# Two layers of attention: difference and band heads among the last input tiles, latent heads among half tiles of the output projection

## The chip, the cores and the metric

The kernel runs on one core of one Trainium2 chip. The metric is the device time of one execution in microseconds (us), as the median of several runs. Its engines are called by their names in the profile: PE is TensorE (PEld its weight loads), DVE VectorE, ACT ScalarE, POOL GpSimd, SP the engine that issues most of the loads. Each has its own queue of instructions, worked off in order.

## The reference

A network of two parts on 256 tokens of width 2048, in float32. The first part has two layers. Of each layer (`first_block`):

```
h = rms_norm(x); proj = h @ w_in              # 30 column tiles of 128: c_q (3), c_kv, k_rope, then q, k, v of B and of C
out_a = mla_mixer(...)                        # 8 latent heads; q and k, v come from c_q @ w_uq and c_kv @ w_ukv
out_b = diff_mixer(...)                       # 4 difference heads, two score maps each, a norm behind them
out_c = chunk_band_mixer(...)                 # 4 band heads with a learned bias
x = x + concat(out_a, out_b, out_c) @ w_o     # output projection, 2048 x 2048
h = rms_norm(x)
x = x + square(relu(h @ w_up)) @ w_down       # 2048 -> 8192 -> 2048
```

The second part (`second_block`) is one layer with a sliding window, a diagonal state space (SSM) and an MLP of the same size. The change doesn't touch its work. The tables of its state space are computed by POOL and ACT beside the two layers of the first part.

## The kernel before

Weights come as chunks of 2 MB (`raw[0]`, `raw[1]`, loaded by SP in turns). A chunk is two tiles. For float32 accuracy every tile is split: ACT copies it into a rounded high part (`w_hi`, two halves of 1024 columns), DVE subtracts to get the low part (`w_lo`), and PE multiplies high by high, high by low and low by high. There are two buffers of high and low parts. So the split of tile T+2 waits on ACT until PE has ended tile T (`tile_done`), and the load of a chunk waits until the chunk before it in its buffer is split.

Of a layer l, in PE's order:

- 30 input tiles (`tile`), whose results DVE folds and scales into `proj` (`project`).
- The "fills": 14 groups of float32 matmuls for w_uq and w_ukv (`uq_done`), read out by ACT (`uq_out`, L1251). Groups 0 to 5 are the long ones. The chunks that follow in the weight buffers wait for them: SP loads chunk 18 (the first of w_o) behind fill 5, chunk 19 behind fill 13.
- 16 transposes of the values of B and C (L810).
- 20 score units in a software pipeline of steps s: units 0 to 7 of the difference heads, 8 to 11 of the band heads, 12 to 19 of the latent heads. PE does `scores(s)`, the transposes of unit s-2 (`turn`), and the product with the values of unit s-3 (`values`). DVE does bias and maxima (`biased`), sums and scaling one step later (`normed`), and the low part of the output five steps later (`act_lo`, L1747). ACT does the exponentials (`exps`, L1264), `weights_out` and the high part of the output (L1280). `values` of a latent head waits for the low part of the output of two heads before (`olo_ready`), since both use one bank of PSUM.
- 16 tiles of the output projection (`wide`), four for each 512 columns, each over a quarter of the rows of w_o. DVE adds each 512 columns to x (`added`, L1577), and PE turns them (`turn_x`, L690) for the next norm.
- The MLP: 16 up tiles and 16 wide down tiles, four times.

Beside this runs the preparation of the SSM. POOL begins `ssm_powers` when all heads of the layer are out (L2056 at its start), and waits in its middle for a sine and cosine that ACT computes in `before_mlp(1)` (L1303 to L1310). `before_mlp(c)` stands in ACT's queue behind the first split that follows the first tile of 512 columns c+1. Behind `ssm_powers` POOL builds the phases (L2172 is the signal that they are ready), then the matrices. Only then does it come to `hidden` (L2207), the low parts of the MLP's hidden tiles. ACT's queue holds this for the MLP:

```
def ffn(T0, c2, H0, each=None, i0=None):
    with act.Fori(0, FCH - 1) as f:
        if i0 is not None:
            ssm_trig_table(i0 + f)            # waits for POOL's phases
        ups(T0, c2, f, H0)
...
def up(T0, c2, f, q, t, H0, to_wide=False):
    T = T0 + 2 * T_UP * f + 4 * q + t
    act.wait_ge(hlo_ready, H0 + T_UP * f + 4 * q + t + 1)   # up tile 2 needs POOL's first hidden tile
    low_to(T, t, hid[t][:])                                 # L1125
...
        split(T + 2, c2 + C_UP * f + q + (t // 2 + 1) // 2, (1 + t // 2) % 2, t % 2)
```

Of the kernel before, what the change touches and what calls it, by code (L numbers as in the profile page):

```python
# [16 lines left out]
F32 = mybir.dt.float32  # L17
# [110 lines left out]
def build(nc, stream, params, tables, tables2, cbias, xrow, gfin, metaT, smat, out, stabs, urow, yrow):  # L128
# [102 lines left out]
    assert side_end <= region[0] - 4 * HC * 384  # L231
# [6 lines left out]
    vb = place("vb", [P, 2, HB * P], where=region)  # L238
    vc = place("vc", [P, 2, HC * P], where=region)
    sb0 = place("sb0", [P, 384], where=region)  # L240
    nmax = [place(f"nmax{i}", [P, 2], where=region) for i in range(2)]
    psums = [place(f"psums{i}", [P, 2], where=region) for i in range(2)]
    rsums = [place(f"rsums{i}", [P, 2], where=region) for i in range(2)]
    nlr = place("nlr", [P, 2], where=region)
    sb = [sb0, sb1]
# [5 lines left out]
    rt = place("rt", [P, 4, 2, S], where=region)  # L251

# [8 lines left out]
    ob, osq, ostd, orstd = proj[:, VB:VB + 4, :], proj[:, VC:VC + 4, :], proj[:, 0:4, :], proj[:, KC:KC + 4, :]  # L261
# [50 lines left out]
    with ExitStack() as ctx:  # L312
# [184 lines left out]

        def gated_tiles(t):

            return [4 * (t // 2) + 2 * e + t % 2 for e in range(2)]  # L500
# [24 lines left out]
        def _(sp):  # L525
# [11 lines left out]
            with sp.Fori(0, DEPTH) as l:  # L537
# [96 lines left out]
        def _(pe):  # L634
# [48 lines left out]

            def turn_x(n, c):
# [83 lines left out]
            with pe.Fori(0, DEPTH) as l:  # L768
# [11 lines left out]
                pe.wait_ge(const_ready, 1)  # L780
                pe.wait_ge(tab_landed, 16)

                pe.wait_ge(cn_ready, l + 1)
# [6 lines left out]
                for n, (c, ws, j0) in enumerate(tiles):  # L790
                    if n in (0, 6, 12):
                        pe.wait_ge(landed[c % 2], chunk_landed(l * C2_LAYER + c // 2))
                    if n % 2 == 0 and n >= 8:
                        pe.wait_ge(uq_out, 14 * l + n // 2 - 3)
                    for k, w in enumerate(ws):
                        last = mm(bank[4 + n // 2 % 4][:, 256 * (n % 2):256 * (n % 2) + 256], w, proj[:, j0 + k, :],
                                  k == 0, k == len(ws) - 1)
                    if n % 2 == 1:
                        last.then_inc(uq_done, 1)
                for g in range(4):  # L800
                    pe.wait_ge(uq_out, 14 * l + 10 + g - 3)
                    c0 = 1024 + 512 * (g % 2)
                    mm(bank[4 + (10 + g) % 4][:], proj[:, QT, 128 * (g // 2):128 * (g // 2) + 128], flat[1][:, c0:c0 + 512], True, True)\
                        .then_inc(uq_done, 1)

                pe.wait_ge(evac_done, evacuated(T0 + T_O - 1))
                pe.wait_ge(uq_out, 14 * l + 14)
                for g, v0 in enumerate((VB, VB, VC, VC)):
                    for h in range(4):
                        last = pe.transpose(bank[4 + g][:, 128 * h:128 * h + 128],  # L810
                                            proj[:, v0 + h, 128 * (g % 2):128 * (g % 2) + 128], ident)
                    last.then_inc(vt_done, 1)

                def scores(u):
# [3 lines left out]
                    else:  # L819
                        pe.wait_ge(vt_out, 4 * l + 4)  # L820
# [19 lines left out]
                def turn(g, u):  # L840
                    pe.wait_ge(pn_ready, GROUPS * l + g + 1)
                    if g >= 2:
                        pe.wait_ge(pt_ready, GROUPS * l + g - 1)
                    for i in range(3):
# [3 lines left out]
                def values(g):  # L848
                    pe.wait_ge(pt_ready, GROUPS * l + g + 1)
                    if 2 <= g < 2 + HB:  # L850
                        pe.wait_ge(osq_ready, HB * l + g - 1)
# [3 lines left out]
                    o = bank[g % 2]  # L855
# [3 lines left out]
                for s in range(UNITS + 3):  # L859
# [1609 lines left out]
```

## Time and profile before

| | |
|---|---|
| median of 3 runs | 3306.08 us (3301.94 to 3314.55) |
| the profiled execution | 3318.74 us |
| its span, first to last instruction | 3316.9 us |
| mean granted clock of PE | 0.973 |
| busy share of the span | PE 98%, DVE 56%, ACT 45%, POOL 19% |
| the chain that ended last | PE 92%, ACT 2%, issue 2%, DVE 2%, DMA 1% |
| head stage of layer 0, last input tile to output projection | 197.25 to 307.07 us |

### The profile page before, as it was taken

Reading aid. Unit: us, or ns where it says so; the run is one execution under the profiler, and the core shown is the slowest. Engines: PE = TensorE matmul, PEld = TensorE weight load, DVE = VectorE, ACT = ScalarE, POOL = GpSimd, SP = SyncE. Lnnn points to the kernel's source line nnn. Section 1 sums busy time; section 2 is a strip of 40 time slices with the busy share of each in tenths; the row PEclk is TensorE's granted clock in tenths of the full one; section 3 lists DMA queues with packets and bytes.
Section 4 is the critical chain, followed back from the end, with each engine's and each line's share of the span. In section 5 each row is a group of like instructions: output and inputs, shape, how many; then the busy total and the mean of one; then the engine's idle time right before and its main releaser. Section 6 shows DMA issues by size and latency. Waiting matters only on the chain.

```text
span 3316.9 us, 46606 instructions
## 1 busy us (share of the span) xinstructions
PE 3235.5 (98%) x16696; PEld 2735.7 (82%) x16696; DVE 1840.9 (56%) x2381; ACT 1493.9 (45%) x2319; POOL 640.7 (19%) x701
## 2 busy tenths in 40 slices
PE   8989999999999999899999999999899999999999
PEld 6877888888888888688888888889866888888887
DVE  5645655565555563656655555557555655555554
ACT  4344553545444443445444444452454544434343
POOL 1011513141411111044414031114110010101010
PEclk9987999999999999699999999999989999999999
DMA  6440456564555545145645555567422455555554
GB/s 227 177 177 34 178 187 223 180 224 182 215 194 211 186 179 190 39 160 181 225 181 210 199 206 203 211 221 261 149 77 102 178 192 189 192 188 195 185 193 162
DMA packets 66281, 602.11 MB, mean 182 GB/s; under 512 B 13968, under 2 KB 24464, under 8 KB 31072
## 3 DMA queue, kind: packets, MB, share of 16 engines
q1 hardware_dynamic: 54560, 592.33, 48.9%
q10 hardware_dynamic: 11184, 5.49, 0.6%
q0 software_dynamic: 400, 2.44, 0.2%
q8 instruction: 87, 1.43, 0.2%
q14 instruction: 50, 0.41, 0.0%
HBM read 582.09 MB, written 18.15 MB: 181 GB/s over the span
## 4 chain that ended last, share of the span: by engine, by line
PE 92%; ACT 2%; issue 2%; DVE 2%; DMA 1%; POOL 0%; SPq 0%; ACTq 0%; DVEq 0%; POOLq 0%
PE bank L638 90%; DMA raw<-stream 1%; PE bank L690 1%; ACT w_hi L1085 0%; DVE w_lo L1534 0%; PE bank L845 0%; DVE w_lo L1528 0%; DMA urow<-us 0%; POOL cssb L2218 0%; DMA u<-urow 0%; PE bank L735 0%; ACT prob L1264 0%; PE bank L970 0%; DVE sb L1714 0%; DVE nmax L1724 0%
## 5 line engine op out<-in xcount | busy, mean ns | idle before, releaser
L638 PE MATMUL bank<-xg,w_hi 128*128 128x512 f32 (+1 forms) x4544 | 1544.7, 387 | 13.8 <-DVE w_lo L1534 10.1
L638 PE MATMUL bank<-xg,w_lo 128*128 128x256 f32 (+1 forms) x4352 | 1228.5, 282 | 0.0
L638 PEld LDWEIGHTS bank<-xg,w_hi 128*128 128x128 f32 x4544 | 849.6, 190 | 195.8 <-DVE w_lo L1534 8.2
L1528 DVE TENSOR_TENSOR w_lo<-raw,w_hi 128x1024 fp32r<-128x1024 f32 x480 | 625.7, 1341 | 520.3 <-ACT w_hi L1096 520.3
L638 PEld LDWEIGHTS bank<-xg,w_lo 128*128 128x128 f32 x4352 | 825.1, 190 | 0.7
L1096 ACT ACTIVATE w_hi<-raw 128x1024 fp32r<-128x1024 f32 x480 | 482.3, 1054 | 660.4 <-PE bank L638 660.4
L1534 DVE TENSOR_TENSOR w_lo<-raw,w_hi 128x1024 fp32r<-128x1024 f32 x548 | 680.2, 1247 | 160.1 <-ACT w_hi L1085 159.7
L638 PE MATMUL bank<-w_hi,act_hi 128*128 128x512 f32 x1920 | 753.5, 392 | 1.9 <-DVE act_lo L1747 1.9
L638 PE MATMUL bank<-w_hi,act_lo 128*128 128x512 f32 x1920 | 749.5, 390 | 0.0
L638 PE MATMUL bank<-w_lo,act_hi 128*128 128x512 f32 x1920 | 749.2, 390 | 0.0
L1085 ACT ACTIVATE w_hi<-raw 128x1024 fp32r<-128x1024 f32 x552 | 552.5, 1052 | 167.5 <-PE bank L638 164.5
L2207 POOL TENSOR_TENSOR act_lo<-hid,act_hi 128x256 f32 x192 | 193.4, 1007 | 1467.8 <-ACT act_hi L1136 1467.8
L638 PEld LDWEIGHTS bank<-w_hi,act_hi 128*128 128x128 f32 x1920 | 361.7, 188 | 82.7 <-issue 6.1
L638 PEld LDWEIGHTS bank<-w_hi,act_lo 128*128 128x128 f32 x1920 | 361.6, 188 | 75.8
L638 PEld LDWEIGHTS bank<-w_lo,act_hi 128*128 128x128 f32 x1920 | 362.0, 189 | 74.0
L1603 DVE TENSOR_TENSOR hid<-bank,hid 128x256 f32<-128x256 f32 x192 | 81.6, 425 | 372.0 <-ACT hid L1125 372.0
L1125 ACT ACTIVATE hid<-bank 128x256 f32<-128x256 f32 x192 | 73.8, 385 | 390.8 <-PE bank L638 390.7
L1136 ACT ACTIVATE act_hi<-hid 128x256 f32 (+1 forms) x192 | 80.6, 420 | 147.8 <-DVE hid L1613 147.8
L1579 DVE SCALAR_TENSOR_TENSOR x<-bank,stats,x 128x512 f32<-128x512 f32 x96 | 67.7, 747 | 90.5 <-issue 77.5
L1125 ACT ACTIVATE proj<-bank 128x256 f32 (+1 forms) x60 | 23.1, 384 | 193.8 <-PE bank L638 193.8
L1603 DVE TENSOR_TENSOR proj<-bank,proj 128x256 f32 (+1 forms) x60 | 25.3, 422 | 111.1 <-ACT proj L1125 110.6
L1613 DVE SCALAR_TENSOR_TENSOR hid<-hid 128x256 f32<-128x256 f32 x192 | 82.9, 432 | 0.0
(311 smaller groups left out, 1934.6 us busy)
## 6 DMA issues: line engine op xcount, KB each, us to landing
raw<-stream SPq DMA_DIRECT2D x264, 2048.0 KB, 7.7
stabs<-ssm_tabs SPq DMA_DIRECT2D x8, 1176.0 KB, 9.8
rdo<-stabs SPq DMA_DIRECT2D x8, 768.0 KB, 8.7
ssm_bc<-smat SPq DMA_DIRECT2D x8, 640.0 KB, 11.9
stabs<-ssm_f SPq DMA_DIRECT2D x8, 512.0 KB, 11.0
drv<-stabs SPq DMA_DIRECT2D x8, 512.0 KB, 5.5
trig<-stabs SPq DMA_DIRECT2D x8, 408.0 KB, 9.7
x<-xrow SPq DMA_DIRECT2D x4, 512.0 KB, 7.2
```

The costliest lines, as they stand in the source:

```text
L638: return pe.matmul(o, a, b, start=start, stop=stop, skip_group_check=True)
L690: last = pe.transpose(bank[4 + k % 4][:, P * m:P * m + P], x[:, m, P * k:P * k + P], ident)
L1085: act.activation(hi[j][:, 8 * h:8 * h + 8, :], raw[r][:, 8 * h:8 * h + 8, P * j:P * j + P], ACT.Copy)\
L1096: act.activation(flat_hi[j][:, 1024 * h:1024 * h + 1024], flat_raw[r][:, 2048 * j + 1024 * h:2048 * j + 1024 * h + 1024], ACT.Copy).then_i ...
L1125: act.activation(dst, bank[b][:, S:2 * S], ACT.Copy).then_inc(low_out, 1)
L1136: act.activation(act_hi[:, bass.ds(4 * q + t, 1), :], hid[t][:].rearrange("p (a n) -> p a n", a=1), ACT.Copy)\
L1528: dve.tensor_tensor(flat_lo[j][:, 1024 * h:1024 * h + 1024], flat_raw[r][:, 2048 * j + 1024 * h:2048 * j + 1024 * h + 1024], flat_hi[j][:, ...
L1534: dve.tensor_tensor(lo[j][:, 8 * h:8 * h + 8, :], raw[r][:, 8 * h:8 * h + 8, P * j:P * j + P], hi[j][:, 8 * h:8 * h + 8, :].bitcast(F32), ...
L1579: dve.scalar_tensor_tensor(out=one, in0=bank[2 * (c % 2) + m][:], scalar=rs2[:, m:m + 1], in1=one, op0=ALU.mult, op1=ALU.add).then_inc(eva ...
L1603: return dve.tensor_tensor(dst, bank[b][:, 0:S], dst, ALU.add).then_inc(folded, 1)
L1613: dve.scalar_tensor_tensor(out=one, in0=one, scalar=0.0, in1=one, op0=ALU.max, op1=ALU.mult).then_inc(evac_done, 1)
L2207: pool.tensor_tensor(act_lo[:, bass.ds(4 * q + t, 1), :], hid[t][:].rearrange("p (a n) -> p a n", a=1), act_hi[:, bass.ds(4 * q + t, 1), : ...
```

## The change

In both layers of the first part the order of the work is written anew. The difference and band units go one by one behind the input tiles 18 to 28, their last steps among the fills. The latent units go among eight tiles of the output projection that need only the rows of the difference and band heads (rows 1024 on), in half tiles (`out_half`) on a list, m counting the latent steps. Eight more tiles for the rows of the latent heads follow, two for each 512 columns, so that each 512 columns are added to x twice. The chunks of w_o are laid out for it on the host. The tiles 18 to 29 and the fills use two banks of PSUM. SP's load of the SSM's matrices moves behind the seventh chunk of w_o. POOL's code is the same, and so are `before_mlp`, `ffn` and `up`.

```diff
+        FILLS = {11: (2,), 12: (3,), 13: (4,), 14: (5,), 15: (6, 7, 8, 9), 16: (10, 11, 12, 13)}
+        OUT_HALVES = {1: (0,), 2: (1,), 3: (2, 3), 4: (4, 5), 5: (6, 7), 6: (8, 9), 7: (10, 11), 8: (12, 13), 9: (14,), 10: (15,)}
+        OUT_SPLITS = {0: 0, 1: 1, 2: 2, 3: 3, 4: 4, 5: 5, 6: 6, 7: 7, 8: 8, 10: 9}
+        OUT_ADDED = {4: 0, 6: 1, 8: 2, 11: 3}
...
-                pair(0, first_matrices)
-                with sp.Fori(0, 7) as q:
-                    pair(2 + 2 * q)
+                pair(0)
+                pair(2)
+                pair(4, first_matrices)
+                with sp.Fori(0, 5) as q:
...
+            def out_half(T, t, h, b, k0):
+
+                pe.wait_ge(lo_ready, lo_count(T, h))
+                for i in (2 * h, 2 * h + 1):
+                    k = k0 + 4 * t + i
+                    for m in range(2):
+                        o = bank[b + m][:]
+                        a_hi, a_lo = (v[:, k, P * m:P * m + P] for v in (act_hi, act_lo))
+                        mm(o, a_hi, wide_hi[t][:, i, :], t == 0 and i == 0, False)
+                        mm(o, a_hi, wide_lo[t][:, i, :], False, False)
+                        last = mm(o, a_lo, wide_hi[t][:, i, :], False, t == 1 and i == 3)
+                if h == 1:
+                    last.then_inc(tile_done, 1)
+
...
-                with pe.Fori(0, 6) as q:
+                with pe.Fori(0, 3) as q:
...
+                def fill(i):
+
+                    if i < 2:
+                        pe.wait_ge(evac_done, evacuated(T0 + T_O - 2 + i))
+                    else:
+                        pe.wait_ge(uq_out, 14 * l + i - 1)
+                    if i == 0:
+                        pe.wait_ge(const_ready, 1)
+                        pe.wait_ge(tab_landed, 16)
+                        pe.wait_ge(cn_ready, l + 1)
+                    if i < 10:
+                        for n in (2 * i, 2 * i + 1):
+                            c, ws, j0 = tiles[n]
+                            if n in (0, 6, 12):
+                                pe.wait_ge(landed[c % 2], chunk_landed(l * C2_LAYER + c // 2))
+                            for k, w in enumerate(ws):
+                                last = mm(bank[i % 2][:, 256 * (n % 2):256 * (n % 2) + 256], w, proj[:, j0 + k, :],
+                                          k == 0, k == len(ws) - 1)
+                    else:
+                        c0 = 1024 + 512 * (i % 2)
+                        last = mm(bank[i % 2][:], proj[:, QT, 128 * ((i - 10) // 2):128 * ((i - 10) // 2) + 128], flat[1][:, c0:c0 + 512],
...
+                for j in range(12):
+                    T = T0 + 18 + j
+                    tile(T, j % 2, j % 2, None, evacuated(T - 2))
+                    if j == 0:
+                        pe.wait_ge(evac_done, evacuated(T0 + VB + 3))
+                        for g in range(2):
+                            turn_values(g)
+                    unit_step(j - 1, 0, MLA0)
+                    if j in (7, 9, 11):
+                        sums((j - 7) // 2)
+                for i in range(2):
+                    fill(i)
+                pe.wait_ge(evac_done, evacuated(T0 + T_O - 1))
+                pe.wait_ge(pt_ready, GROUPS * l + 5)
...
+                for s in range(11, 17):
+                    if s == 12:
+                        sums(3)
+                    unit_step(s, 0, MLA0)
+                    for i in FILLS[s]:
+                        fill(i)
...
+                for m in range(UNITS - MLA0 + 3):
+                    unit_step(MLA0 + m, MLA0, UNITS)
+                    for w in OUT_HALVES.get(m, ()):
+                        if w in (0, 1):
+                            pe.wait_ge(onlo_ready, HB * l + 2 * w + 2)
+                        if w == 0:
+                            pe.wait_ge(ostd_ready, 5 * l + HB)
+                            pe.wait_ge(olo_ready, OTHERS * l + HC)
+                        elif w % 4 == 0:
+                            pe.wait_ge(evac_done, evacuated(T0 + T_O + w // 2 - 1))
+                        out_half(T0 + T_O + w // 2, w // 2 % 2, w % 2, 2, 8)
+
+                pe.wait_ge(pt_ready, GROUPS * l + GROUPS)
+                for c in range(NC):
+                    if c % 2:
+                        pe.wait_ge(evac_done, evacuated(T0 + T_O + 8 + 2 * c - 3))
+                    for t in range(2):
+                        for h in range(2):
+                            if c == 0:
+                                pe.wait_ge(olo_ready, OTHERS * l + HC + 4 * t + 2 * h + 2)
+                            out_half(T0 + T_O + 8 + 2 * c + t, t, h, 2 * (c % 2) if c else 6, 0)
+                        if c and t == 0:
+                            pe.wait_ge(evac_done, evacuated(T0 + T_O + 8 + 2 * c - 1))
+                            turn_x(2 * l + 1, c - 1)
                 ffn(T0 + T_FFN, l * H_LAYER, 2 * l + 1, 2 * l + 2, FCH * l)
...
+                for m in range(UNITS - MLA0 + 4):
+                    unit_step(MLA0 + m, MLA0, UNITS)
+                    if m in OUT_SPLITS:
+                        out_split(OUT_SPLITS[m])
+                    if m == 0:
+                        for h in range(HB):
+                            act.wait_ge(on_ready, HB * l + h + 1)
+                            act.activation(act_hi[:, 8 + h, :], ob[:, h, :], ACT.Copy).then_inc(onhi_ready, 1)
...
-                widened(T0 + T_O, c0 + 9, before_mlp)
+                for c in range(NC):
+                    for t in range(2):
+                        i = 8 + 2 * c + t + 2
+                        (split_wide if i < 16 else split)(T0 + T_O + i, c0 + 9 + i // 4, i // 2 % 2, t)
+                        if c and t == 0:
+                            before_mlp(c - 1)
+                before_mlp(NC - 1)
...
+                def unit_step(s, a, b):
+
+                    if max(a, CB0) <= s - 5 < b:
+                        output_low(s - 5)
+                    if s - MLA0 in OUT_ADDED and a == MLA0:
+                        c = OUT_ADDED[s - MLA0]
+                        half_added(T0 + T_O + 2 * c + 1, c, 2)
+                    if a <= s < b:
+                        if s == CB0:
+                            dve.wait_ge(cb_landed, 16 * l + 16)
                         biased(s)
-                    if 1 <= s < UNITS + 1:
+                    if a <= s - 1 < b:
...
+                for m in range(UNITS - MLA0 + 5):
+                    unit_step(MLA0 + m, MLA0, UNITS)
+                    if m in OUT_SPLITS:
+                        out_split(OUT_SPLITS[m])
+                    if m == 0:
+                        for h in range(HB):
+                            normed_low(h)
...
-                widened(T0 + T_O, lambda c: gained(2 * l + 1, c, "mlp_g", l * KT))
+                for c in range(NC):
+                    for t in range(2):
+                        T = T0 + T_O + 8 + 2 * c + t
+                        i = 8 + 2 * c + t + 2
+                        if t == 1:
+                            half_added(T, c, 2 * (c % 2) if c else 6)
+                        for h in range(2):
+                            if i < 16:
+                                split_wide_half(T + 2, i // 2 % 2, t, h)
+                            else:
+                                split_half(T + 2, i // 2 % 2, t, h)
+                            if c == NC - 1 and t == 1 and h == 0:
+                                gained(2 * l + 1, NC - 1, "mlp_g", l * KT)
+                        if c and t == 0:
+                            gained(2 * l + 1, c - 1, "mlp_g", l * KT)
```

## Rows read from the trace of the kernel before

**Rows 1.** The page's second part, TensorE's clock in 40 slices, in tenths.

```profile
PEclk9987999999999999699999999999989999999999
```

**Rows 2.** The windows, 20 us, layer 0 (PE, PEld, DVE, ACT, POOL, clock, DMA, GB/s).

```profile
280.00:300.00 20.00, 20.00 (x58) 13.69 (x56) 13.56 (x30) 6.14 (x24) 0.00 (x0) 0.50 0.00 1
```

**Rows 3.** The timeline of PE, layer 0 (start, us, engine, line, operation).

```profile
220.87 1.97 PE L810 MATMUL bank<-tab,proj 128*128 128x128 f32 x16 [0.69 <-ACT va L1251]
...
238.61 1.65 PE L638 MATMUL bank<-proj 64*128 64x128 f32 x4
...
260.97 0.39 PE L638 MATMUL bank<-kn,qn 128*128 128x128 f32 x2
...
263.61 0.55 PE L845 MATMUL bank<-tab,prob 128*128 128x128 f32 x3
...
264.00 0.82 PE L638 MATMUL bank<-probT,vc 128*128 128x256 f32 x4
...
264.65 1.89 PE L638 MATMUL bank<-proj,ones 128*128 128x256 f32 x8
...
307.07 0.50 PE L638 MATMUL bank<-w_hi,act_hi 128*128 128x512 f32 x1 [0.93 <-DVE act_lo L1747]
```

**Rows 4.** The timeline of ACT, layer 0, input and head stages.

```profile
197.25 0.38 ACT L1125 ACTIVATE proj<-bank 128x256 f32<-128x256 f32 x1 [5.20 <-PE bank L638]
...
212.79 0.60 ACT L1251 ACTIVATE qn<-bank 128x512 f32<-128x512 f32 x1 [1.99 <-PE bank L638]
...
234.09 0.19 ACT L1264 ACTIVATION_READ_ACCUMULATOR prob<-sb,nmax 128x1 f32 x1
```

**Rows 5.** The timeline of DVE, same stretch.

```profile
232.06 0.55 DVE L1714 SCALAR_TENSOR_TENSOR sb<-tab,bank 128x384 f32<-128x384 f32 x1
```

**Rows 6.** The instructions of tile act_lo (ns minimum/median/maximum).

```profile
L1747 DVE TENSOR_TENSOR act_lo<-bank,act_hi x24: 417/424/426, 262.9 to 1408.7; 128x256 fp32r<-128x256 f32 x24
```

**Rows 7.** The page's sixth part: issues, KB, us to landing.

```profile
raw<-stream SPq DMA_DIRECT2D x264, 2048.0 KB, 7.7
```

**Rows 8.** The timeline of PE, second block, at a wait.

```profile
2456.91 0.90 PE L970 MATMUL bank<-tab,prob 128*128 128x128 f32 x3 [2.36 <-DVE prob L1971]
```

**Rows 9.** The windows, 2.5 us, behind that wait.

```profile
2457.50:2460.00 2.50, 2.50 (x11) 1.14 (x10) 2.12 (x8) 1.61 (x7) 0.84 (x3) 0.50 0.95 406
```

**Rows 10.** The timeline of ACT, layer 0, output projection and first up tiles.

```profile
357.29 2.01 ACT L1096 ACTIVATE w_hi<-raw 128x1024 fp32r<-128x1024 f32 x2 [3.43 <-PE bank L638]
...
379.94 2.01 ACT L1096 ACTIVATE w_hi<-raw 128x1024 fp32r<-128x1024 f32 x2 [3.44 <-PE bank L638]
...
386.30 2.01 ACT L1096 ACTIVATE w_hi<-raw 128x1024 fp32r<-128x1024 f32 x2 [1.68 <-PE bank L638]
...
404.75 1.28 ACT L1163 ACT_TABLE_LOAD   x1
...
417.06 0.39 ACT L1125 ACTIVATE hid<-bank 128x256 f32<-128x256 f32 x1 [0.47 <-PE bank L638]
```

**Rows 11.** The timeline of DVE, output projection.

```profile
358.38 2.36 DVE L1528 TENSOR_TENSOR w_lo<-raw,w_hi 128x1024 fp32r<-128x1024 f32 x2 [2.91 <-ACT w_hi L1096]
...
374.57 1.29 DVE L1577 TENSOR_TENSOR x<-bank,x 128x512 f32<-128x512 f32 x2 [1.91 <-PE bank L638]
```

**Rows 12.** The timeline of PE, third up tile.

```profile
411.16 0.50 PE L638 MATMUL bank<-xg,w_hi 128*128 128x512 f32 x1 [1.62 <-DVE w_lo L1534]
```

**Rows 13.** The timeline of POOL, output projection, up tiles, and one later build.

```profile
307.10 0.56 POOL L2056 TENSOR_TENSOR ssm_t<-par 128x32 f32<-128x32 f32 x2 [95.49 <-DVE act_lo L1747]
...
361.31 0.26 POOL L2056 TENSOR_TENSOR ssm_lpow<-ssm_mag,ssm_cs 128x32 f32<-128x32 f32 x1 [41.97 <-ACT ssm_cs L1310]
...
389.42 1.06 POOL L2172 COPY consts<-consts 128x1 f32<-128x1 f32 x1
...
413.87 0.74 POOL L2207 TENSOR_TENSOR act_lo<-hid,act_hi 128x256 f32 x1
...
515.11 0.19 POOL L2172 COPY consts<-consts 128x1 f32<-128x1 f32 x1
```

More of the change, by code:

```diff
@@ L789, in _ @@
                 tiles += [(17, [flat[1][:, 128 * t:128 * t + 128]], QT) for t in range(HA)]
[L790 to L808, printed above, removed]
+                def fill(i):
[18 more added lines that the diff above has]
+                        last = mm(bank[i % 2][:], proj[:, QT, 128 * ((i - 10) // 2):128 * ((i - 10) // 2) + 128], flat[1][:, c0:c0 + 512],
+                                  True, True)
+                    last.then_inc(uq_done, 1)
@@ new lines, in _ @@
+                for j in range(12):
+                    project(18 + j, j % 2)
+                    if j < 10:
+                        split(T0 + 20 + j, c0 + (20 + j) // 4, (20 + j) // 2 % 2, j % 2)
+                    if j == 0:
+                        for g in range(2):
+                            values_turned(g)
+                    unit_step(j - 1, 0, MLA0)
+                    if j in (8, 10):
+                        sums_out((j - 8) // 2)
+                for i in range(2):
+                    fill_out(i)
@@ new lines, in _ @@
+                for g in range(2, 4):
+                    values_turned(g)
+                sums_out(2)
+                for s in range(11, 17):
+                    if s == 12:
+                        sums_out(3)
+                    unit_step(s, 0, MLA0)
+                    if s == 13:
+                        act.wait_ge(ostd_ready, 5 * l + HB)
+                        act.activation(ostd, ostd, ACT.Sqrt, bias=eps, scale=1.0 / P).then_inc(ostd_ready, 1)
+                    for i in FILLS[s]:
+                        fill_out(i)
@@ new lines, in normed_low, with out_split, half_added @@
+                def normed_low(h):
+                    dve.wait_ge(onhi_ready, HB * l + h + 1)
+                    dve.tensor_tensor(act_lo[:, 8 + h, :], ob[:, h, :], act_hi[:, 8 + h, :].bitcast(F32), ALU.subtract)\
+                        .then_inc(onlo_ready, 1)
+                def out_split(i):
+                    for h in range(2):
+                        split_wide_half(T0 + T_O + i, i // 2 % 2, i % 2, h)
+                def half_added(T, c, b):
+                    dve.wait_ge(tile_done, multiplied(T))
+                    for m in range(2):
+                        one = x[:, m, W * c:W * c + W]
+                        dve.tensor_tensor(one, bank[b + m][:], one, ALU.add).then_inc(evac_done, 1)
```

209 lines of the change are left out of this document (94 added, 115 removed).

## The prediction

> **What bounds the kernel now.** I read the page's busy shares first, then TensorE's clock beside them, then the windows and timelines of the stages the diff touches. PE is the chain: outside two stretches it is dense and its clock is full. The clock in slices [rows 1] shows two dips, in the third and fourth slices and in the 17th, which are the head stages of the two layers. In the second half of the latent units PE is busy for all 20 us of a window and gets 0.50, the 1.2 GHz level [rows 2]. So the busy share hides the loss: work lies there that costs twice. The stage lasts from the last input tile (197.25 [rows 4]) to the first tile of the output projection (307.07 [rows 3]), 109.8 us. The projection behind it goes without a gap.
>
> **What the stage holds at full clock.** Fills: from 197.25 to 220.18, the end of ACT's last read-out in front of the transposes (220.87 less the idle 0.69 [rows 3]), 22.9. Transposes 2.0 [rows 3]. One latent step, scores 2.64 (260.97 to 263.61), transposes 0.39, values 0.65, is 3.68, eight of them 29.4 [rows 3]. A difference score took 1.65 at the lower level [rows 3], so 0.83; eight of these with four transposes and values make 11. Four band units, a score as dear, 7.4. The sums of the norm 1.9 [rows 3]. Sum 74.6. Hidden gaplessly between tiles that PE runs anyway, the change would take 109.8 - 74.6 = 35.2 us off each layer. I charge 2 for some 20 more switches between kinds of work at about 0.1.
>
> **Input stage.** Behind each of 11 tiles (5.58 apart: 5.20 idle and 0.38 on ACT [rows 4]) stands one unit, 1.2 to 1.9 on PE. A split holds ACT for 2.0 [rows 10] and DVE until 3.45 after a tile's end (358.38 + 2.36 - 357.29 [rows 10, 11]); with fold, scaling, bias, maxima and one unit's sums DVE is done some 6.4 after it, inside 7 to 7.5. The next split is ready a whole tile ahead. I expect no stall. Two banks in place of four hold too, since a tile's bank is free before its neighbour ends.
>
> **First half of the projection, step by step.** A tile is 5.43 and a turn of x 0.93: four tiles and one turn lie between 357.29 and 379.94, one of each between 379.94 and 386.30 [rows 10]. A half is 2.72. I count from the end of the last fill.
>
> Junction, m=0 and 1. PE does two scores, to 5.3. Its first half tile needs, in a row: scores 2.64; bias to exponentials 2.2 (232.06 to 234.28 [rows 4, 5]); then, because `out_split(0)` stands behind `exps(12)` in ACT's queue, the split, 3.45; then two low parts of difference heads behind it on DVE, 0.7. That is 9.0, so PE idles 3.7. Chunk 18 is no later: it is asked for behind fill 5, lands in 7.7 [rows 7], and the eight fills after take about 7.4 (212.79 to 220.18 [rows 4]). An idle of 2.36 in the second block [rows 8] was followed by a window at 0.50 [rows 9]; restarting I charge 2.5 here. Junction 6.2.
>
> Steps m=4 to 9. The split of tile w+2 waits for the end of tile w, and in DVE's queue it stands ahead of the next step's work. So after each step's last half tile DVE is free at 3.45, has the low part of a head at 3.87 (0.42 [rows 6]) and an addition to x at 5.16 (1.29 [rows 11]). PE wants the low part when scores and transposes are done, at 3.03, and the addition (before halves 4, 8, 12) after values.
> - m=4: addition at 4.74 against 3.68: 1.1.
> - m=5 and 7: 0.85 each.
> - m=6: 0.85, values to 4.52, addition 5.16: 1.5.
> - m=8: no scores are left, PE asks at 0.39: 3.5, values to 4.5, addition 5.16: 4.1.
> - m=9: 3.5, because `out_split(8)` has DVE again.
> Together 11.9, and 2 for the clock behind the two long gaps. Steps 10 and the latent half of the projection I cost at nothing: there splits (3.45) and additions (1.29) fit in a tile of 5.43. If DVE slipped there by more than 0.7, each slip would show on PE.
>
> The saving is 35.2 - 2 - 6.2 - 13.9 = 13.1 per layer. The eight additions more, 1.29 each, cost only what stands above.
>
> **What the diff doesn't touch but moves.** `before_mlp(1)` still stands behind the first tile of the third 512 columns. Before, seven tiles of the projection are left then; now the columns have two tiles, and three are left. Relative to the end of the projection, E (379.94 + 0.93 + 3 x 5.43 = 397.16 [rows 10]), sine and cosine come four tiles later, 21.7. What hangs on them:
> - POOL starts again at 361.31, 35.9 before E, signals the phases at 390.48 and is free for `hidden` at 413.87, 52.6 after its start [rows 13]. It will start 14.1 before E.
> - ACT wants the phases at 404.75, E+7.6 [rows 10]: the cover was 14.3. Moved unchanged they come at E+15.
> - Up tile 2 wants POOL's first hidden tile at 417.06 [rows 10]; it is there at 414.6, a cover of 2.4. Moved unchanged it is there at E+39.2.
> POOL needn't be so long: its signal took 1.06 in this stretch and 0.19 in another [rows 13], beside DVE's splits. Nine operations of such a length lie behind the phases' start, 0.87 apiece; DVE stands idle while PE waits, so I give back 5.5 and keep 0 and 8.1 as ends. Hidden tile 0 is then ready at E+33.7. Behind it: ACT 0.39, split half 1.05, DVE half 1.2, so up tile 4 starts at E+36.3. Before, tile 2 started at 411.16 [rows 12], E+14.0, and tile 4 two tiles of 5.6 later, E+25.2. The loss is 11.1, and 1.8 for a cold start: 12.9 per layer. On the way ACT's wait for the phases opens the gap in front of up tile 2 from 1.62 to about 7, inside the same sum. POOL's first part, 12.2 long (307.10 to 319.3, [rows 13]), still ends well ahead of the cosine.
>
> The Trainium skill says of POOL's slow operations (SBUF — State Buffer, "Who interferes with whom") that a DVE instruction with two SBUF inputs contends with a GpSimd instruction that reads SBUF, and that the one that comes second waits for the whole of the first. The signal's 1.06 against 0.19 agrees.
>
> **Sum.** 13.1 gained, 12.9 lost, twice: -0.4 us. The profiled execution would go from 3318.7 to 3318.3. It lies 12.7 above the median of the runs shown, by which the forecast is 3306.
>
> **Rivals.**
> - A, the preparation stays hidden. For it: POOL might be much faster beside an idle DVE. Against: 21.7 us against covers of 14.3 and 2.4. The loss of 12.9 falls away: 3306 - 26 = 3280.
> - B, the queues in steps 4 to 9 don't bite, since DVE or ACT run ahead of my order. For it: in the second block, head steps among half tiles leave PE few gaps. Against: the waits are in the order of the queues. 13.9 less: 3278.
> - C, the slower side: the clock. In the old stage the latent units never brought it back alone [rows 2]. If the idle at the junction puts PE to 1.2 GHz and m=1 to 3 all stay there, the half of m=1 costs 2.7 more, m=2 5.7 (scores, transposes, half), m=3 9.1: 17.5, where I charged 2.5. That is 15 per layer, 3336. It decides from 8.3 us per layer on, about two such steps. The Trainium skill (TensorE: Matmul & The Clock Gate, "HAM oscillation — how this bites in real kernels") tells of kernels whose bursts alternate with waits and start cold every time, which is this rival; the dip behind the wait in the second block agrees, and the full clock of the slices after it [rows 1] speaks against its lasting.
> - D, POOL isn't shortened: 5.5 more per layer, 3317, inside the middle.
> - E, both A and B and no junction, 66 off: 3240.
>
> **Numbers.** The forecast with D 0.45, A 0.13, B 0.13, E 0.04, C 0.16, and 0.09 for a lag in the input stage that no row shows. Its own range is 3294 to 3319: per layer POOL's ends give +5.5 and -2.6, the clock charges (2.5, 2 and 1.8, each between 0 and twice) up to 3 or so either way. With A and B on one side and C on the other, 3278 to 3336. A measurement of this kernel can tell about 0.5%, 16.5 us. Faster 0.30 (A, B, E), same 0.45, slower 0.25.
>
> **What would show it.** The head units among the input tiles without PE idle; the clock at 1.00 there. An idle of 3 to 4 in front of the first half tile of w_o. In steps 8 and 9 two gaps of 3 to 4 ended by `act_lo`. ACT waiting for POOL at the first table of the MLP, and up tile 4 starting 35 to 38 us after the end of the projection, in both layers. I am wrong if that time stays near 25, if the eight first tiles and units take far from 93 us (29.4 + 8 x 5.43 + 6.2 + 13.9) from the last fill, or if the clock is low through the latent steps.

## The result and the profile after

| | before | changed |
|---|---|---|
| median, 13 runs each, side by side | 3304.64 us (3292.72 to 3315.91) | 3320.98 us (3312.94 to 3324.87) |
| profiled execution | 3318.74 us | 3324.87 us |
| mean granted clock in it | 0.973 | 0.980 |

The ratio is 1.0041 [1.0027, 1.0055]: slower by 16 us, where I forecast no change. Forty-three more runs of the kernel before, beside the experiments, put its median over 56 runs at 3306.1 us. The profiled executions differ by 6.1 us only; the forecast was -0.4 for them. So there are two things to explain: 6.5 us in the sum for the profiled executions, and some 9 us more by which the medians lie apart (the changed kernel's median is 3.9 below its profiled execution, that of the kernel before 12.7).

PE's clock in 40 slices, the changed kernel. The dip to 6 of [rows 1] is gone:

```profile
PEclk9998999999999999999999999999989999999999
```

PE's timeline in layer 0, every wait from the first half tile of w_o to up tile 4 (the idle time in brackets):

```profile
251.34 0.79 PE L651 MATMUL bank<-w_hi,act_hi 128*128 128x512 f32 x1 [3.62 <-DVE act_lo L1865]
...
276.96 0.49 PE L651 MATMUL bank<-w_hi,act_hi 128*128 128x512 f32 x1 [1.14 <-DVE x L1878]
...
286.57 0.92 PE L651 MATMUL bank<-probT,va 128*128 128x256 f32 x4 [0.85 <-DVE act_lo L1836]
...
296.85 0.92 PE L651 MATMUL bank<-probT,va 128*128 128x256 f32 x4 [0.85 <-DVE act_lo L1836]
...
298.12 0.49 PE L651 MATMUL bank<-w_hi,act_hi 128*128 128x512 f32 x1 [0.35 <-DVE x L1878]
...
309.32 1.65 PE L651 MATMUL bank<-probT,va 128*128 128x256 f32 x4 [0.86 <-DVE act_lo L1836]
...
320.96 0.92 PE L651 MATMUL bank<-probT,va 128*128 128x256 f32 x4 [3.54 <-DVE act_lo L1836]
...
322.24 0.66 PE L651 MATMUL bank<-w_hi,act_hi 128*128 128x512 f32 x1 [0.37 <-DVE x L1878]
...
333.45 1.65 PE L651 MATMUL bank<-probT,va 128*128 128x256 f32 x4 [3.54 <-DVE act_lo L1836]
...
406.83 0.80 PE L651 MATMUL bank<-xg,w_hi 128*128 128x512 f32 x1 [4.92 <-DVE w_lo L1632]
...
426.88 0.80 PE L651 MATMUL bank<-xg,w_hi 128*128 128x512 f32 x1 [6.64 <-DVE w_lo L1632]
```

These rows answer to [rows 3] and [rows 12]. The reader is to see the junction (3.62; I had 3.7), the steps m=4 to 9 (1.14, 0.85, 0.85 and 0.35, 0.86, 3.54 and 0.37, 3.54, together 11.5; I had 11.9), and two waits at the MLP's start where [rows 12] has one of 1.62. The windows of the same phase (length, PE busy, clock, DMA share, GB/s) show what the idle sums don't:

```profile
242.00:252.00 10.00, 6.38 (x27) 0.77 0.57 210
252.00:262.00 10.00, 10.00 (x36) 0.72 0.37 123
...
282.00:292.00 10.00, 9.14 (x44) 1.00 0.06 23
292.00:302.00 10.00, 8.79 (x34) 0.83 0.44 152
302.00:312.00 10.00, 9.14 (x38) 0.84 0.13 57
...
322.00:332.00 10.00, 7.66 (x27) 0.83 0.47 190
332.00:342.00 10.00, 8.55 (x27) 0.66 0.01 2
342.00:352.00 10.00, 10.00 (x45) 1.00 0.40 132
```

ACT's timeline, layer 0: the last fill read out, the split behind the eighth tile, which ends the first half, the split at the projection's end E (in [rows 10] this is at 397.16 by the count, 7.5 later), and the wait for the phases:

```profile
242.34 0.60 ACT L1307 ACTIVATE va<-bank 128x512 f32<-128x512 f32 x1 [0.36 <-PE bank L651]
...
343.40 2.01 ACT L1155 ACTIVATE w_hi<-raw 128x1024 fp32r<-128x1024 f32 x2 [7.88 <-PE bank L651]
...
389.63 2.01 ACT L1144 ACTIVATE w_hi<-raw 128x1024 fp32r<-128x1024 f32 x2 [1.65 <-PE bank L651]
...
401.73 0.43 ACT L1222 ACTIVATE ssm_turn_n<-ssm_phase 128x272 f32<-128x272 f32 x1 [4.09 <-POOL consts L2320]
```

From 242.34 to 343.40 are 101.1 us, where I wrote 93. POOL's timeline, against [rows 13]: it starts, waits 11.09 for the cosine, begins again at E-14.1, gives its signal in 0.19, and is free for the hidden tiles at E+33.8:

```profile
348.79 0.56 POOL L2204 TENSOR_TENSOR ssm_t<-par 128x32 f32<-128x32 f32 x2 [121.07 <-DVE act_lo L1836]
...
375.53 0.26 POOL L2204 TENSOR_TENSOR ssm_lpow<-ssm_mag,ssm_cs 128x32 f32<-128x32 f32 x1 [11.09 <-ACT ssm_cs L1402]
...
401.51 0.19 POOL L2320 COPY consts<-consts 128x1 f32<-128x1 f32 x1
...
423.41 1.40 POOL L2355 TENSOR_TENSOR act_lo<-hid,act_hi 128x256 f32 x2 [0.23 <-issue]
```

### The profile page after: what moved, and what is told of

It is laid out like the page before. It is cut to its first block, busy times and chain, and to the rows that moved or that the text cites. A ratio compares the mean times of both kernels' runs of the same rounds, so it can differ in the third digit from the quotient of the medians.

```text
span 3323.1 us, 46580 instructions
## 1 busy us (share of the span) xinstructions
PE 3216.0 (97%) x16696; PEld 2721.5 (82%) x16696; DVE 1845.9 (56%) x2397; ACT 1495.0 (45%) x2325; POOL 639.4 (19%) x701
## 4 chain that ended last, share of the span: by engine, by line
PE 89%; POOL 3%; issue 3%; ACT 2%; DVE 2%; DMA 1%; SPq 0%; DVEq 0%; ACTq 0%; POOLq 0%
PE bank L651 88%; ACT w_hi L1155 1%; ACT w_hi L1144 0%; POOL ssm_tabs L2295 0%; DVE w_lo L1626 0%; PE bank L717 0%; DMA raw<-stream 0%; POOL ssm_t L2204 0%; DMA urow<-us 0%; POOL cssb L2366 0%; PE bank L881 0%; DMA u<-urow 0%; DVE x L1878 0%; PE bank L762 0%; DVE w_lo L1632 0%
## 5 line engine op out<-in xcount | busy, mean ns | idle before, releaser
L651 PE MATMUL bank<-w_hi,act_hi 128*128 128x512 f32 x1920 | 762.5, 397 | 11.1 <-DVE act_lo L1865 7.4
L1184 ACT ACTIVATE proj<-bank 128x256 f32<-128x256 f32 (+1 forms) x60 | 22.9, 382 | 140.5 <-PE bank L651 140.5
L1701 DVE TENSOR_TENSOR proj<-bank,proj 128x256 f32<-128x256 f32 (+1 forms) x60 | 25.3, 421 | 96.8 <-ACT proj L1184 96.4
## 6 DMA issues: line engine op xcount, KB each, us to landing
stabs<-ssm_f SPq DMA_DIRECT2D x8, 512.0 KB, 10.9
```

The lines of the kernel that those rows point to most:

```text
L651: return pe.matmul(o, a, b, start=start, stop=stop, skip_group_check=True)
L1184: act.activation(dst, bank[b][:, S:2 * S], ACT.Copy).then_inc(low_out, 1)
L1701: return dve.tensor_tensor(dst, bank[b][:, 0:S], dst, ALU.add).then_inc(folded, 1)
```

## The experiments

The theory after this reading: the change loses at three separate places, each an order in a queue that can be put right alone: (a) the late sine and cosine, (b) DVE's splits ahead of the low parts and additions in steps 4 to 9, (c) `out_split(0)` behind the first latent unit. The rivals are in each expectation. Each median is of 5 to 12 runs. The intervals are of the ratio to the kernel before on the same chip; its own median among these groups of runs went from 3296 to 3309, so I compare the medians of the kernels themselves with 3321.0.

**The sine two tiles of w_o earlier.** In the changed kernel's `before_mlp`:

```
-                    if c == 1:
+                    if c == 0:
```

> The changed kernel with ACT's sine and cosine one group of 512 columns earlier: before_mlp(0) in place of before_mlp(1), two tiles and a turn of x, some 11.8 us, further ahead of the projection's end E. Theory: some 14 us per layer are lost at the start of the MLP because POOL starts on the cosine only at E-14.1. Its first part ended at 364.45 and it waited 11.1 us for ACT, so it should now start about 10 us earlier, have hidden tile 0 at about E+24 instead of E+33.8, and up tile 4 should start near E+28 instead of E+37.3: 9 to 11 us per layer, 18 to 22 us in all, 3299 to 3303. Rival: the MLP's start is bound by something else (splits, weights); then E to up tile 4 stays at 37 and the time within 3 us of the changed kernel's.

Measured: 3308.1 us (3302.7 to 3312.0), ratio 1.0003 [0.9990, 1.0017]; 12.8 less than the changed kernel. Its PE timeline has E at 386.26 (first up tile) and up tile 4 29.5 behind it, where the changed kernel has 389.43 and 37.5:

```profile
386.26 0.40 PE L651 MATMUL bank<-xg,w_hi 128*128 128x512 f32 x1
...
415.73 0.80 PE L651 MATMUL bank<-xg,w_hi 128*128 128x512 f32 x1 [3.43 <-DVE w_lo L1632]
```

By these rows 8.0 per layer come back, 16 in the two layers; in the medians it is 12.8 in all. Both are less than the 18 to 22 I expected. The rival falls: the MLP's start did wait for the preparation. E itself is 3.2 earlier here, though nothing ahead of it was edited; that is how far two executions lie apart.

**The same lateness in the kernel before.** Only the sine is moved, four tiles later:

```
-                    if c == 1:
+                    if c == 2:
```

> The kernel before, with ACT's sine and cosine two groups of 512 columns later (before_mlp(2)), which puts them as far ahead of E as the change does; nothing else is changed. Theory: this alone costs what the MLP's start lost in the change, 14 us per layer, 26 to 29 in all: the profile should show up tile 4 near E+37 instead of E+25.2, and a time 0.8% to 0.9% above the kernel before. Rival: POOL catches up and the preparation stays hidden (rival A of the prediction): within 3 us of before. Rival: POOL isn't shortened by the quieter DVE, or the loss depends on the half tiles: some 20 per layer or more.

Measured: 3332.5 us (3327.6 to 3342.3), ratio 1.0079 [1.0060, 1.0097], 25 to 26 above the kernel before. PE's timeline:

```profile
390.44 0.40 PE L638 MATMUL bank<-xg,w_hi 128*128 128x512 f32 x1
...
408.65 0.79 PE L638 MATMUL bank<-xg,w_hi 128*128 128x512 f32 x1 [5.63 <-DVE w_lo L1534]
...
428.71 0.80 PE L638 MATMUL bank<-xg,w_hi 128*128 128x512 f32 x1 [7.08 <-DVE w_lo L1534]
```

Up tile 4 starts 38.3 behind the first. Without half tiles or moved heads the lateness alone costs what I had charged, 13 per layer. The prediction's rival A, a preparation that stays hidden, falls.

**DVE's splits one step later.** In the changed kernel, `out_split(m)` of DVE moves behind the low part and the addition of step m+1:

```
 def unit_step(s, a, b):
     if max(a, CB0) <= s - 5 < b:
         output_low(s - 5)
     if s - MLA0 in OUT_ADDED and a == MLA0:
         ...
+    if a == MLA0 and s - MLA0 - 1 in OUT_SPLITS and s > MLA0 + 1:
+        out_split(OUT_SPLITS[s - MLA0 - 1])
     if a <= s < b:
...
-    if m in OUT_SPLITS:
+    if m == 0:
         out_split(OUT_SPLITS[m])
```

> The changed kernel with DVE's part of out_split(m) moved one latent step later, behind output_low and half_added of that step and ahead of its bias. Theory: PE's idle at steps m=4 to 9 (11.6 us in layer 0, ended by act_lo L1836 and by x L1878) is the order of DVE's queue, and the half-speed windows behind the idles are its consequence. Expected: these idles fall to 1 us or less in all, the clock stays at 1.00 from m=2 on, and each layer gains 11 of idle and up to 8 of clock: 15 to 19 per layer, 30 to 38 in all, 3283 to 3291. Rival 1: the clock is low for another reason (the small matmuls themselves, in bursts): then only the 11 us of idle per layer come back, 3299. Rival 2: the low parts and additions are late by themselves, not by the splits ahead of them: no gain.

Measured: 3286.9 us (3276.9 to 3290.0), ratio 0.9931 [0.9913, 0.9949]; 34 less than the changed kernel, and faster than the kernel before. What PE waited for from 240 to 450 us (total, times, longest):

```profile
PE bank L651 <- DVE w_lo L1632: 11.1, 2, 6.1
PE bank L651 <- DVE act_lo L1867: 3.8, 1, 3.8
PE bank L651 <- DVE x L1880: 0.5, 1, 0.5
PE bank L651 <- DVE act_lo L1836: 0.2, 1, 0.2
```

The waits at steps 4 to 9 fell from 11.5 to 0.7, and all windows from 262 us to the end of the projection are at 1.00. From the last fill to the end of the eighth tile this profile takes 80.1 us in layer 0 and 79.7 in layer 1, where the changed kernel took 101.1 and 98.5. Of the 21.0 and 18.8 us saved, 10.9 and 11.1 are idle time; the other 10.1 and 7.7 are clock. Both rivals fall: the order of the queue made these waits, and the low clock of these steps went with them.

**The first split ahead of the first latent unit.** DVE's loop is shown; on ACT `out_split(0)` and the high copies of the difference heads move in the same way:

```
+    if m == 0:
+        out_split(0)
+        for h in range(HB):
+            normed_low(h)
     unit_step(MLA0 + m, MLA0, UNITS)
-    if m in OUT_SPLITS:
+    if m and m in OUT_SPLITS:
         out_split(OUT_SPLITS[m])
-    if m == 0:
-        for h in range(HB):
-            normed_low(h)
```

> The changed kernel with out_split(0) and the high and low copies of the difference heads ahead of the first latent unit's bias and exponentials, on ACT and DVE. Theory: PE's idle of 3.6 us in front of the first half tile of w_o, and the window at 0.50 behind it, come from out_split(0) standing behind exps(12). Expected: the idle falls from 3.6 to under 1.5 us (the split is then ready 3.5 to 4 us after the last fill and PE has 5.3 us of scores), and the half-speed window goes with it: 3 to 6 per layer, 6 to 12 in all, 3309 to 3315. Rival: the chunk of weights lands late, or the wait for the difference heads sets the start: the idle stays, no gain.

Measured: 3312.7 us (3303.2 to 3318.0), ratio 1.0020 [1.0006, 1.0035], 8.3 less. The junction's idle is gone altogether; its window shows the unexpected part:

```profile
242.00:252.00 10.00, 10.00 (x32) 0.69 0.54 210
```

PE is busy for all ten microseconds and the clock is low all the same. So an idle isn't needed for a low clock around the junction, and what I had charged isn't the price of the idle alone. Over the 20 us from the last fill's read-out the clock was 0.74 or 0.83 in the twelve stretches profiled with the junction's idle, and 0.83, 0.91, 1.00, 0.91, 1.00 and 0.91 in the six without it, in both layers of this kernel and of two more below. Outside the idle itself that is a loss of 1.6 to 3.4 us, 2.5 on the mean, against 0 to 3.4, 1.4 on the mean: the idle may add a microsecond, no more.

**Pairs, and all three.**

> The changed kernel with the early split of tile 0 and DVE's later splits, without the early sine. Alone they took 8 and 34 us off the changed kernel's 3321, which adds up to 3279; the three edits together took 73 where their sum is 55, so 18 us come from two or three of them meeting. Theory: the 18 us are clock. In the three edits' profile the clock is 1.00 from 242 us on, where each edit alone still has 0.69 to 0.77 in the first 10 us of the phase; with the junction and the waits behind it gone PE has no idle left between the fills and the end of the projection, so most of the 18 belongs to this pair: 3260 to 3268. Rival: it belongs to the early sine (a start of the MLP at full clock): then 3276 to 3282 here.

> The changed kernel with DVE's later splits and the early sine, without the early split. Alone they took 34 and 13 us off 3321, which adds up to 3274. Theory (the 18 us of the three edits beyond their sum belong to the gapless first half): the junction's idle of 3.8 us and a window near 0.76 behind it are still there, and the time is 3270 to 3277. Rival (they belong to the early sine, whose shorter waits at the start of the MLP no longer lower the clock when more time is left): up tile 4 starts near E+28 at 1.00 and the time is 3254 to 3262.

> The changed kernel with all three edits of before: out_split(0) and the copies of the difference heads ahead of the first latent unit, DVE's splits one step later, and the sine and cosine at before_mlp(0). Theory: the three losses are separate. The edits alone took 8, 34 and 13 us off the changed kernel's 3321; added up that is 3266, and I expect 3262 to 3274, 1.0% to 1.3% under the kernel before. Rival: the early sine gives more with the others than alone or nothing at all, since POOL's first part starts when the latent heads end and all three meet there; then 3275 to 3287. With the projection dense, PE in layer 0 should be at 1.00 from about 260 us to its end, and up tile 4 at about E+29.5.

| kernel | median us | ratio to before | off 3321.0 | sum of the single edits |
|---|---|---|---|---|
| first split and DVE's order | 3269.8 (3267.0 to 3281.8) | 0.9923 [0.9895, 0.9951] | 51 | 42 |
| DVE's order and sine | 3258.2 (3251.8 to 3261.1) | 0.9875 [0.9849, 0.9901] | 63 | 47 |
| all three | 3248.0 (3242.8 to 3258.3) | 0.9824 [0.9801, 0.9846] | 73 | 55 |

The version with all three is the fastest, 1.8% below the kernel before. My expectation for it (3262 to 3274) was too high by 14 or more, and its rival's too. The column "off 3321.0" compares groups on different chips, and the kernel before itself ran at 3296.4 beside the pairs and at 3307.3 beside the single edits. By the ratios the pairs gain 39 and 55, where the single edits add up to 43 and 49, and all three gain 72 for a sum of 56. So the surplus of a pair is uncertain by some 10 us. What holds is the comparison of the pairs, which ran side by side: the one with the sine is 11.6 faster, and 5 of that is its larger sum, so it has some 7 more of surplus. Its time fits the rival's range (3254 to 3262), while the other pair's 3269.8 lies between its two ranges. The theory that the surplus belongs to the dense first half has the runs against it. The PE timelines of all three and of the pair with the sine, at the MLP's start:

```profile
359.73 0.40 PE L651 MATMUL bank<-xg,w_hi 128*128 128x512 f32 x1
...
373.44 0.51 PE L651 MATMUL bank<-xg,w_hi 128*128 128x512 f32 x1 [1.24 <-DVE w_lo L1633]
...
387.59 0.50 PE L651 MATMUL bank<-xg,w_hi 128*128 128x512 f32 x1 [2.31 <-DVE w_lo L1633]
```

```profile
379.57 0.50 PE L651 MATMUL bank<-xg,w_hi 128*128 128x512 f32 x1 [1.24 <-DVE w_lo L1632]
...
393.72 0.50 PE L651 MATMUL bank<-xg,w_hi 128*128 128x512 f32 x1 [2.32 <-DVE w_lo L1632]
```

Up tile 4 comes 27.9 behind the first in place of 29.5 (POOL now begins earlier relative to E, since the stage in front is shorter), and in these rows, of layer 0, its first matmul takes 0.50, not 0.80. Counted from E until the tiles run evenly again, the early sine alone gives 7.4 and 8.5 back in the two layers, and 11.8 and 10.1 with the two other edits: 6 of the surplus of 18. Another 6, by these profiles, lie at a place that no edit touches (below). The last 6 I can't assign.

**Copies.** What differs between executions of one kernel? Three more of the kernel before, and two of the changed one:

> The kernel before, unchanged, for another profile of it. Question: where do its own executions differ (3292 to 3316, in step with the mean granted clock, 0.983 to 0.974)? Theory: in the head stages of the two layers, from the last input tile to the first tile of w_o, which took 109.8 us in both layers of the profiled execution before. If this execution is a fast one (clock 0.98 or more), at least one of its stages should take 98 to 104 us, with windows at 1.00 in the latent units; the time outside the two stages should agree within 2 us. Rival: the difference is spread over the kernel, and both stages take 109.8 again.

> The kernel before once more, as the copy a: for each execution, its time less the length of its two head stages should be the same within 2 us by the theory; by the rival the stages are alike and the rest varies.

> The kernel before once more, as the copies a and b: the two head stages carry the whole difference between its executions by the theory; by the rival they carry none of it.

> The changed kernel, unchanged, for another profile of it. Open: the kernel before has places at two levels of the clock, its two head stages (103.5 to 104.6 or 109.5 to 109.9 us) and the stretch from the first up tiles of layer 1 to the wait behind the state space's transposes at the start of the second block (from up tile 4 on, 886 to 888 us or some 877 to 880). The change rebuilds only the first two. Theory: the changed kernel's first half of the output projection keeps to a narrow range, 98 to 102 us from the last fill to tile 8, and the untouched third place still takes either level, 887 or 877 to 882. Rival: the third place is always at its slow level in the changed kernel, whatever the execution, and that is part of why it is slower.

> The changed kernel once more, as its copy a, with the same question: 98 to 102 us from the last fill to tile 8 in both layers, and 887 or 877 to 882 us from up tile 4 of layer 1 to the wait at the start of the second block.

Worked out from the timelines (head stage: last input tile on ACT to the first tile of w_o on PE; third place: up tile 4 of layer 1 to a wait of 2.36 at the start of the second block; for the kernel before up tile 2 and 11.2 more stand for tile 4):

```
execution                 time      clock  head stage 0 and 1   third place
before, profiled          3318.74   0.973  109.8   109.9        886.9
before, copy a            3313.54   0.974  109.5   109.7        885.5
before, copy b            3292.71   0.983  104.6   103.5        879.3
before, copy c            3300.23   0.979  109.7   103.5        876.8
before, late sine         3336.17   0.974  103.6   109.7        886.8
changed, profiled         3324.87   0.980    -       -          887.6
changed, copy a           3315.89   0.982    -       -          879.7
changed, copy b           3316.65   0.981    -       -          879.5
all three edits           3246.04   0.992    -       -          881.4
```

Rows of copy b that the table rests on, ACT's and then PE's, in layer 0 and 1:

```profile
194.29 0.38 ACT L1125 ACTIVATE proj<-bank 128x256 f32<-128x256 f32 x1 [5.20 <-PE bank L638]
...
1286.69 0.38 ACT L1125 ACTIVATE proj<-bank 128x256 f32<-128x256 f32 x1 [5.20 <-PE bank L638]
```

```profile
298.91 0.50 PE L638 MATMUL bank<-w_hi,act_hi 128*128 128x512 f32 x1 [0.93 <-DVE act_lo L1747]
...
1390.21 0.50 PE L638 MATMUL bank<-w_hi,act_hi 128*128 128x512 f32 x1 [0.93 <-DVE act_lo L1747]
```

And the windows of the third place, the profiled kernel before and its copy c:

```profile
2233.27:2278.27 45.00, 39.45 (x290) 0.87 0.68 231
```

```profile
2225.13:2270.13 45.00, 44.48 (x362) 0.99 0.82 277
```

The theory, that the head stages carry the whole difference, is half right. The same instructions take 109.5 to 109.9 or 103.5 to 104.6 us there, in step with the clock. But they carry 11.5 of the 26 us between the profiled execution and copy b; the third place carries 7.5, and the rest lies at the start and ahead of layer 1's head stage. From the wait at the third place to the end both kernels take 905.3 to 906.1 us in every profile. The rival of the last two copies falls: the changed kernel too has the third place at either level. Its phase from the last fill to the end of the eighth tile stayed in 98 to 101 us.

At the third place it isn't the clock alone. PE waits there for a small load, 136 KB of the state space's input `u`, which ACT issues next to one of SP's 2 MB loads of weights. The profiled kernel before (SP, ACT, PE), then its copy c (ACT, SP, PE):

```profile
2242.98 0.33 SPq L530 DMA_DIRECT2D raw<-stream  x1
2243.21 0.34 ACTq L1347 DMA_DIRECT2D u<-urow  x1
2251.06 3.68 PE L638 MATMUL bank<-u,drv 128*128 128x68 f32 x16 [5.54 <-DMA u<-urow]
```

```profile
2233.97 0.34 ACTq L1347 DMA_DIRECT2D u<-urow  x1
2234.72 0.33 SPq L530 DMA_DIRECT2D raw<-stream  x1
2237.09 1.90 PE L638 MATMUL bank<-u,drv 128*128 128x68 f32 x16
```

In the seven of the fourteen profiles with a slow third place (885 to 888 us) the weights were issued up to 0.9 us ahead of `u` (in one 0.01 behind it), `u` landed after 7.1 to 8.2 us, and PE waited 5.5 to 5.7 for it; its matmuls behind the wait shown take 3.68 in place of 1.90. In the seven quick ones the weights came 0.6 to 1.5 us behind `u`, which landed after 2.0 to 2.6, and PE didn't wait for this first one, and for the next one 1.5 at most. All fourteen profiles agree with the order of the two issues as the cause. It isn't shown, since no run moves either of them.

## Why the prediction was wrong

**The input stage: right.** No idle among the input tiles, the clock at 1.00 from 120 to 240 us. The last fill is read out 45.1 after [rows 4]'s last input tile; the working makes it 47.2, and 0.7 of the difference lies at the kernel's start.

**Junction and queue waits: right in place and size, wrong in what the clock adds.** The idle came to 15.1 against 15.6 of the sum. The work itself, 29.4 and 43.4 in the sum, is 74.1 in the profile of all three edits, where the same phase runs at 1.00 with 0.5 of idle. So the clock cost 101.1 less 74.1 and 15.1, that is 11.9 in layer 0, and 9.1 in layer 1 (98.5 for the phase), where I charged 2.5 and 2. This is the term of the sum that was mis-sized, by 7.4 and 4.6. It is rival C at less than half its size, and for the most part at another place: of the clock that is missing in layer 0, 5.1 us lie in the windows from 242 to 262 us around the junction, 1.8 of them inside its idle, so that my 2.5 was near; and 8.5 lie in those from 292 to 342, around the gaps of steps 5 to 9, for which I had charged 2. The experiment with DVE's order shows it: with 11 us of idle, 10.1 and 7.7 of clock went. The Trainium skill (TensorE: Matmul & The Clock Gate, "HAM oscillation — how this bites in real kernels"), which I weighed for C, tells of work in bursts that starts cold behind each wait. The windows behind the waits of 3.5 agree (0.83 and 0.66 from 322 to 342 us); between those of 1.14 and 0.85 the clock stayed at 1.00 (282 to 292), and the window without any idle at 0.69 it does not explain.

**The MLP's start: right.** POOL began at E-14.1 as worked out, was free at E+33.8 (E+33.7), and up tile 4 started at E+37.3 (E+36.3); with a first tile of 8.0 in place of 5.6 the loss is 14.3 in layer 0 and 14.4 in layer 1, for 12.9. POOL was shortened as I had it, so D falls with A.

**The sum.** E came 7.6 earlier in layer 0, and in layer 1 13.8 counted from the state left by layer 0, for 13.1 each. Of the 13.8, 4.4 were gained among the first input tiles of layer 1, which the change doesn't touch; the profiled execution before was slow there, as its copy c was, while copies a and b were 2.9 and 4.4 quicker. Twice 13.1 - 12.9 was forecast, and 7.6 - 14.3 + 13.8 - 14.4 = -7.3 came; the rest of the kernel gave 1.2 back. So I was too low by 12.0 for the clock and by 2.9 for the MLP. 4.4 of that came back in that stretch, 0.7 at the kernel's start, and some 2 in smaller waits and the second halves of the projection. The stretch is luck of the one execution: without it the sum would have been off by 11 in place of 6.5.

**The step that failed for the median.** "It lies 12.7 above the median of the runs shown, by which the forecast is 3306." This took the excess of the profiled execution to be a constant that any version of the kernel carries. It is not: the changed kernel's own profiled execution lies 3.9 above its median, 8.8 less. Part of the excess lies in the very stage that the change takes apart. The 35.2 us of cover contain the slow level of both head stages, which four of ten head stages profiled did not have, at some 6 us each: 2.4 on the mean, 5 for the two of an execution. The median of the kernel before never had all of the loss that the change removes, so the gain is smaller for it by about 5; this is an estimate from five profiles. With the 6.1 between the profiled executions it leaves some 4 of the 15 us between the medians open: how often each kernel meets the slow level at the third place and elsewhere, so few profiles can't say. Neither failed step alone would have put the time outside the range of 3294 to 3319: the clock in the queue waits, with all else that the sum missed, is 6.5 us and gives 3313; the excess is 8.8 and gives 3315. The two together did. That the sum's 3318.3 for the profiled execution is close to the measured median of 3321.0 is chance, for the profiled execution took 3324.9.

"Outside two stretches it is dense" was wrong too: the profiled kernel before waits 5.5 us for `u` at the third place. Of rivals, B fell (the queues bit as listed) and E with it.

## What to carry to other kernels

When a profiled execution lies above the median, look for where its excess is before carrying it through a forecast: if the change rebuilds that place, the excess does not survive. Moving a block of work past others moves everything that hangs on its queue; here three orderings of single instructions, the sine on ACT, the splits on DVE and one split at the junction, turned 15 us of loss into 58 of gain. Idle time that a queue puts in front of PE can cost more than itself when it comes in a stretch of alternating small work: here 11 us of waits per layer were 21 and 19 us in the two layers' profiles, and 17 per layer in the medians.

## What the runs showed of the hardware

- The same instructions ran at different clocks in different executions: 20 us in the latent units of the kernel before at 0.50 with PE busy throughout [rows 2], and the same units in copy b at 0.66 (277 to 297 us) and, in its layer 1, at 0.84 (1369 to 1389). In the kernel before time and mean clock go together: 3313 to 3316 us at 0.974 to 0.976, 3291 to 3293 at 0.983. What decides for one level in the head stages stays open.
- The clock can be low without an idle in front, as in the kernel with the early split: 0.69 from 242 to 252 us with PE busy throughout; with DVE's later splits added, which change nothing before step 2, the same stretch ran at 1.00, in one profile of each of two kernels. Layer 1 of all three kernels had 0.91 over its first 20 us.
- A load of 136 KB took 7.1 to 8.2 us to land when a load of 2 MB from another queue was issued with it or up to 0.9 us before, and 2.0 to 2.6 us when that came 0.6 us or more behind (fourteen profiles).
- A wait of 4.9 in front of an up tile was followed by a first matmul of 0.8 in every profile, and one of 1.2 by 0.5. In between, the length of the wait doesn't decide: the waits of 3.43 and 2.32 shown above gave 0.80 and 0.50, but in layer 1 of the same two runs waits of 3.72 and 2.60 gave 0.50 and 0.79.
